# Two blocks of transformers in fp32: the order of the gate and up products of 256 tokens, and where the context's modulation is summed

## The reference

```python
def swiglu_ffn(h, w_in, w_out):
    gate, up = jnp.split(h @ w_in, 2, axis=-1)
    return (jax.nn.silu(gate) * up) @ w_out
...
    for l in range(DEPTH):
        x = x + FFN_RESID * swiglu_ffn(rms_norm(x, ffn1_norm[l]), ffn1_w_in[l], ffn1_w_out[l])
...
        x = x + FFN_RESID * swiglu_ffn(rms_norm(x, ffn2_norm[l]), ffn2_w_in[l], ffn2_w_out[l])
...
    s_c = jax.nn.silu(c)
    s_cc = jax.nn.silu(c_ctx)[None]
    for i in range(DEPTH):
        ml = (s_c @ w_mod[i] + b_mod[i]).reshape(-1, 3, 3, D)
        mc = (s_cc @ w_mod[i] + b_mod[i]).reshape(-1, 3, 3, D)
```

## Time and profile before

| | us |
|---|---|
| median of 3 runs | 3210.66 (3208.84 to 3212.32) |
| the profiled execution | 3210.62 |
| its span, first to last instruction | 3208.8 |
| PE busy | 3145.6, 98% |
| DVE busy | 1988.8, 62% |
| ACT busy | 1360.5, 42% |
| POOL busy | 129.1, 4% |
| granted TensorE clock, mean | 0.995 |

### The profile page before, as it was taken

One profiled execution on the slowest core, in us unless ns is written; L12 is line 12 of the kernel. 1 busy time (PEld: TensorE's weight loads), 2 busy tenths in 40 slices (PEclk: granted clock), 3 DMA queues, 4 the chain that ended last, 5 costly groups with the idle time before them and its releaser, 6 DMA issues.

```text
span 3208.8 us, 39761 instructions
## 1 busy us (share of the span) xinstructions
PE 3145.6 (98%) x15550; PEld 2625.7 (82%) x15550; DVE 1988.8 (62%) x2775; ACT 1360.5 (42%) x1907; POOL 129.1 (4%) x160
## 2 busy tenths in 40 slices
PE   8999999999999999999999999999999999999998
PEld 7888888888888887888878888788887788887787
DVE  7968778778687787763344444776335643345665
ACT  6546655455566555322233333323223322245553
POOL 1000000000000000000000000300000000021000
PEclk9999999999999999999999999999999999999999
DMA  8755366667554676542332222354324633253354
GB/s 255 246 192 180 124 197 223 223 224 242 162 182 135 201 237 205 190 157 93 105 99 79 79 92 80 105 171 152 111 92 158 211 117 106 91 139 91 105 188 154
DMA packets 334901, 496.78 MB, mean 155 GB/s; under 512 B 11042, under 2 KB 221884, under 8 KB 334716
## 3 DMA queue, kind: packets, MB, share of 16 engines
q1 hardware_dynamic: 330652, 483.46, 45.5%
q0 software_dynamic: 4064, 10.77, 1.5%
HBM read 493.09 MB, written 1.10 MB: 154 GB/s over the span
## 4 chain that ended last, share of the span: by engine, by line
PE 94%; DVE 3%; issue 1%; ACT 1%; DMA 0%; POOL 0%; SPq 0%; DVEq 0%; POOLq 0%; ACTq 0%
PE bank L567 23%; PE bank L569 23%; PE bank L568 23%; PE bank L623 13%; PE bank L624 7%; PE bank L582 1%; PE bank L738 1%; PE bank L753 0%; PE bank L1032 0%; DVE wlo L1715 0%; DMA raw<-in_w_in_dram 0%; DVE bank L2550 0%; PE bank L590 0%; POOL small L2618 0%; ACT npr L1663 0%
## 5 line engine op out<-in xcount | busy, mean ns | idle before, releaser
L1715 DVE TENSOR_TENSOR wlo<-raw,whi 128x1024 fp32r<-128x1024 f32 (+1 forms) x780 | 940.0, 1213 | 899.2 <-ACT whi L1198 896.9
L1198 ACT ACTIVATE whi<-raw 128x1024 fp32r<-128x1024 f32 (+1 forms) x780 | 815.7, 1050 | 1154.1 <-PE bank L569 990.3
L623 PE MATMUL bank<-xT,whi 128*128 128x512 f32 x1760 | 621.8, 398 | 1.5 <-DVE xT L1796 1.0
L567 PE MATMUL bank<-xTh,whi 128*128 128x512 f32 (+1 forms) x1312 | 509.0, 388 | 6.9 <-DVE xTl L1796 6.7
L569 PE MATMUL bank<-xTh,wlo 128*128 128x512 f32 (+1 forms) x1312 | 505.0, 385 | 0.0
L568 PE MATMUL bank<-xTl,whi 128*128 128x512 f32 (+1 forms) x1312 | 504.8, 385 | 0.0
L624 PE MATMUL bank<-xT,wlo 128*128 128x256 f32 x1760 | 496.2, 282 | 0.0
L623 PEld LDWEIGHTS bank<-xT,whi 128*128 128x128 f32 x1760 | 333.1, 189 | 82.1 <-issue 3.4
L567 PE MATMUL bank<-whi,hh 128*128 128x512 f32 x968 | 378.3, 391 | 0.0
L569 PE MATMUL bank<-whi,hl 128*128 128x512 f32 x968 | 377.2, 390 | 0.0
L568 PE MATMUL bank<-wlo,hh 128*128 128x512 f32 x968 | 377.0, 389 | 0.0
(11 more groups left out here) (383 smaller groups left out, 3653.0 us busy)
## 6 DMA issues: line engine op xcount, KB each, us to landing
raw<-in_ffn_w_in_dram SPq DMA_DIRECT2D x176, 1024.0 KB, 5.2
raw<-in_ffn_w_out_dram SPq DMA_DIRECT2D x80, 1024.0 KB, 5.1
mraw<-in_w_mod_dram SPq DMA_DIRECT2D x72, 1024.0 KB, 5.1
raw<-in_w_in_dram SPq DMA_DIRECT2D x44, 1024.0 KB, 5.2
raw<-in_ret_w_in_dram SPq DMA_DIRECT2D x24, 1024.0 KB, 5.1
raw<-in_w_branch_dram SPq DMA_DIRECT2D x12, 1024.0 KB, 5.1
raw<-in_nat_w_qkv_dram SPq DMA_DIRECT2D x12, 1024.0 KB, 5.2
raw<-in_ffn_w_out_dram SPq DMA_DIRECT2D x16, 512.0 KB, 3.4
```

The costliest lines, as they stand in the source:

```text
L567: pe.matmul(ps, lh, rh, start=start, stop=False, skip_group_check=True)
L623: pe.matmul(ps[:, :], wh[:, k, :], x, start=k == 0, stop=False, skip_group_check=True)
L1198: nc.scalar.activation(hi, src, ACT.Copy).then_inc(*e.inc("hi", key, part))
L1715: nc.vector.tensor_tensor(lo, src, hi.bitcast(F32), ALU.subtract).then_inc(*e.inc("lo", key, part))
```

## The change

It does two things. In `feature_pairs` a part's eight 512-column products (`mm_high`, which waits for whi alone) now come before its eight 256-column ones (`mm_low`, ahead of which PE waits for wlo); with `norm` all high products of both parts come as xT arrives, then the low ones of one part and of the other. And in f1 and f2 VectorE accumulates only `who` 0 of the modulation, in one place per step (`mod_steps`, after `ahead`). For `who` 1 ScalarE multiplies (k = 0 straight into `macc`, else into a new buffer `mprod`) and GpSimd adds. TensorE's sums wait for both (`mod_step`, `mod_other`), SP's modulation loads for both readers. The adds are put into GpSimd's list after the norm of f1 (before the one of the mixers) and after that of f2.

```diff
+        mprod = arena("mprod", [P, D], 24 * KB)
...
                             sp.wait_ge(*e.at("mod_read", q - 2))
+                            if mods.halves[q - 2][0][0][0] == "f":
+                                sp.wait_ge(*e.at("mod_read_too", q - 2))
...
                     pe.wait_ge(*e.at("mod_step", c, KD - 1))
+                    if name[0][0] == "f":
+                        pe.wait_ge(*e.at("mod_other", c, KD - 1))
...
-                order = [(mc, k) for mc in range(2) for k in range(KD)]
+
+                def begun(mc):
+                    pe.wait_ge(*e.at("hi", key, mc))
+                    w[mc] = part_views(key, mc)[1:]
+                    ps[mc] = new(*u, mc, ring="pairs")
+
                 if norm:
                     order = [(0, 0), (0, 1), (1, 0), (1, 1)] + [(mc, k) for k in range(2, KD) for mc in range(2)]
-                for mc, k in order:
-                    if norm and mc == 0:
-                        pe.wait_ge(*e.at("xT", norm, k))
-                    if mc not in w:
-                        w[mc] = split_ready(key, mc)
-                        ps[mc] = new(*u, mc, ring="pairs")
-                    m = mm2(ps[mc], k, *w[mc])
-                    if k == KD - 1 and mc == 0:
+                    for mc, k in order:
+                        if mc == 0:
+                            pe.wait_ge(*e.at("xT", norm, k))
+                        if mc not in w:
+                            begun(mc)
+                        mm_high(ps[mc], k, w[mc][0])
+                for mc in range(2):
+                    if not norm:
+                        begun(mc)
+                        for k in range(KD):
+                            mm_high(ps[mc], k, w[mc][0])
+                    pe.wait_ge(*e.at("lo", key, mc))
+                    for k in range(KD):
+                        m = mm_low(ps[mc], k, w[mc][1])
+                    if mc == 0:
                         m.then_inc(*e.inc("used", key, mc))
-                    elif k == KD - 1:
+                    else:
                         m.then_inc(*e.inc(*u, also=[("used", key, mc)]))
...
+            def mod_products(name, at):
+
+                for c, k, q in mods.steps.get((name, at), ()):
+                    act.wait_ge(mod_landed[q % 2], 16 * (q // 2 + 1))
+                    if c + k == 0:
+                        act.wait_ge(*e.at("scc"))
+                    read = [("mod_read_too", q)] if k % 2 else []
+                    if k == 0:
+                        if c >= 2:
+                            act.wait_ge(*e.at("modp", c - 2))
+                        A(macc[c % 2][:, 1, :], mraw[q % 2][:, 0, :], ACT.Copy, scale=scc[:, k, 1:2])\
+                            .then_inc(*e.inc("mod_other", c, 0))
+                    else:
+                        if k > 1:
+                            act.wait_ge(*e.at("mod_other", c, k - 1))
+                        elif c:
+                            act.wait_ge(*e.at("mod_other", c - 1, KD - 1))
+                        A(mprod[:, :], mraw[q % 2][:, k % 2, :], ACT.Copy, scale=scc[:, k, 1:2])\
+                            .then_inc(*e.inc("mod_product", c, k, also=read))
+
...
                         high(g - 1)
+                    mod_products(name, 2 * g)
...
                     A(sg[:, g % 2, :], sg[:, g % 2, :], ACT.Silu).then_inc(*e.inc("sg", name, g, 0))
+                    mod_products(name, 2 * g + 1)
...
                         down_ahead(until, name, n, d)
+                        if name[0][0] == "f":
+                            mod_products(name, 22 + 6 * n + d)
...
-                    for who in whos_of(c):
+                    for who in range(1) if name[0][0] == "f" else whos_of(c):
                         a, wk, s = macc[c % 2][:, who, :], mraw[q % 2][:, k % 2, :], scc[:, k, who:who + 1]
...
-                    mod_half(name, 2 * g, 0)
+                    mod_steps(name, 2 * g)
...
-                    mod_half(name, 2 * g, 1)
                     ahead(until, (name, "up", g))
-                    mod_half(name, 2 * g + 1, 0)
+                    mod_steps(name, 2 * g + 1)
...
                     behind(until, (name, "up", g))
-                    mod_half(name, 2 * g + 1, 1)
...
+            def mod_other(c):
+
+                for k in range(1, KD):
+                    pool.wait_ge(*e.at("mod_product", c, k))
+                    pool.wait_ge(*e.at("mod_other", c, k - 1))
+                    a = macc[c % 2][:, 1, :]
+                    nc.gpsimd.tensor_tensor(a, a, mprod[:, :], ALU.add).then_inc(*e.inc("mod_other", c, k))
+
...
                     norm(("f1", l), 256)
+                for c in MOD_PARTS["f1", l]:
+                    mod_other(c)
                 norm(("mx", l), 256)
...
                 norm(("f2", l), 256)
+                for c in MOD_PARTS["f2", l]:
+                    mod_other(c)
```

More of the change, by code:

```diff
@@ L618, in feature_major_arriving, with mm_high, mm_low @@
                                 m.then_inc(*e.inc(*also[0]))
-            def mm2(ps, k, wh, wl):
+            def mm_high(ps, k, wh):
                 x = xT256[:, k, :, :].rearrange("p a t -> p (a t)")
                 pe.matmul(ps[:, :], wh[:, k, :], x, start=k == 0, stop=False, skip_group_check=True)
+            def mm_low(ps, k, wl):
                 return pe.matmul(ps[:, 256:512], wl[:, k, :], xT256[:, k, 0, :], start=False, stop=k == KD - 1,
@@ L1830, in turned_y @@
                             m.then_inc(*e.inc("yT", name, c, frees=("ty", name, u) if j == n - 1 else None))
[L1832 to L1847, removed]
             def mod_steps(name, at):
```

## The result

| | before | after |
|---|---|---|
| median, us | 3209.97 (3205.09 to 3213.18, 9 runs) | 3217.34 (3216.78 to 3219.91, 9 runs) |
| span of the profiled execution, us | 3208.8 | 3215.5 |
| VectorE busy, us | 1988.8 | 2018.9 |
| ScalarE busy, us | 1360.5 | 1425.2 |
| GpSimd busy, us | 129.1 | 293.9 |

The change makes the kernel slower: ratio 1.0027, 95% interval 1.0018 to 1.0035. The forecast was 3212 us; the time lies in the range of 3204 to 3221, on the side of rival (c). VectorE, which gave away 64 instructions, is busier than before.

The account below looks back on a forecast made before the run. TensorE was taken to bound the kernel, over 94% of the span, so only its products' pitch could yield time. 0 - 4.6 + 5.9 + 0 = +1.3 us on 3210.6 us gave 3212 us, range 3204 to 3221.

Parts of the forecast that it names:

- rival (c): f1 and f2, slabs 22 to 27: GpSimd's adds make wlo late, L624 or L569 waiting; 3224 us, 20%.
- VectorE gives work away, GpSimd adds: Modulation sums in f1 and f2: 78 us off VectorE and 56 adds of 2.4 us on GpSimd, priced at 0.
- The sum is 5.9 us behind: Slabs 20 to 26: VectorE falls back 0.7 us in five down slabs, 1.25 us in two gate and up slabs.
- cover: Lead of a wlo: 3 parts of 2.72 us less 1.06 and 1.22 us, 5.9 us, judged just enough.
- the bound: If a 0.69 us VectorE instruction doesn't overlap the add in two slabs: 1.4 us in four FFNs, 5.6 us.
- The order of the products: 220 parts: 27 ns lost per change from 256 to 512 columns, 0 for the reverse, 5.9 us lost.
- The slow rhythm: About 690 alternating pairs in f2 of layer 0, f1 of layer 1: 6.6 ns each, 4.6 us gained by blocks.
- The later wait for lo: PE asks for lo 1.8 us later: taken as 0, up to 0.5 us at each of five FFN starts.
- ScalarE's products: 64 products of 1024 columns at 1.15 us, 74 us in all, expected to lie in ScalarE's idle time.
- SP's and PE's new waits: SP waits for ScalarE's mraw reads, PE's sum for the last add: SP no later, the add 11 us ahead.
- the half-clock stretches: After the norms: one stretch costs about 1.7 us, and two more or less are possible either way.
- No wait of PE on wlo: Sign of a right forecast: PE waits on none of wlo, macc or whi in the five FFNs.

Follow-up runs that it names:

- the kernel with short adds: The changed kernel with each GpSimd add on 64 of 1024 columns, ScalarE's products and all waits kept: 3209.25 us, ratio 1.0004 to the kernel before.
- the order alone: The kernel before with only the new order of products, the modulation sums staying on VectorE: 3209.32 us, ratio 1.0002 to the kernel before.

## Why the prediction was right or wrong

**The number: in the range, by the width of the range.** The sum gave 1.3 us more than before; the medians differ by 7.4. The range held the time because it was drawn as far as rival (c), and (c), at 20%, is what happened.

**VectorE gives work away, GpSimd adds: wrong, and this is the step that failed**, in "The sum is 5.9 us behind", "5.9 us" of cover, "It just fits. I take 0". The mechanism, the instructions that it strikes, the place (slabs 22 to 27) and the sign (a product of the down stage waiting for wlo; it was L570, L567 before, and not the L569 that I named) were all there, as rival (c). The term itself was mis-sized: nothing in the sum, 7.4 us measured. Both sides of the balance were missed. The cover is 5.6 us (the kernel with short adds). The backlog is 7.0: without the stall PE would have read the part at 158.84 + 0.23 = 159.07, the split ended at 160.5, 1.4 us too late, and 5.6 us of lead were gone. I had spread the holds evenly, one to a slab of 5.44 us, 0.7 us behind each. The accumulations start at 140.53, 148.06, 155.90 and 161.57 us, 7.5, 7.8 and 5.7 us apart, 4.7 us behind in three slabs where I had 2.1. The first interval still holds the last group's sum, product and hl; the second has two holds, since ScalarE made its next product at 150.51, as soon as GpSimd was free, and two adds started 3.7 us apart. The price is 1.8 to 1.9 us at each of four places, 7.4, against 0 in the sum and 5.6 as the bound. A balance of two numbers that are equal to a tenth is no reason for 0: a miss on either side costs, and none gains.

**The order of the products: mechanism right, size 1.5 us off.** From 256 to 512 columns 27 ns was right (1.84 us for eight against 8 x 0.2267). From 512 to 256, where I took 0 and excluded a gain, the eight take 0.95 us against 0.96, and sixteen 1.91 against 1.92: 7 ns are won. 20 ns x 220 = 4.4 us instead of 5.9.

**The slow rhythm: right that blocks don't fall into it; wrong to book it as a property of two FFNs.** In the profile before it cost 4.6 us; in another execution it lies elsewhere, in a similar number of pairs, so the 4.6 us are an estimate from one draw. Its gain and the price of the widths nearly cancel, and the order alone agrees with that (ratio 1.0002). One correction to my rows: the earlier trace rows stand in f2 of layer 0 (f1 of layer 1 begins only at 647 us); the pair of FFNs named in the text is the right one.

**The later wait for lo, ScalarE's products, SP's and PE's new waits: right**, nothing in time that can be measured. The products take 1.13 us (I took 1.15). ScalarE waited 2.7 us for GpSimd, in 4 places; an add that comes first lasts 2.4 us, as I took.

**What would show it**: the parts of 2.80 us, the eights at 0.227 and 0.120 us, the lengths of wlo and of the adds came as forecast. "No wait of PE on wlo" did not, and the sign named for (c) is the row that appeared. (c) gave 3217.6 us for the late wlo alone; the time is 3217.34. That the two are so close is partly luck: the stalls cost 1.8 us more than (c) had them, the widths 1.5 and the half-clock stretches 1.2 us less.

## What to carry to other kernels

Before work is moved from VectorE to GpSimd, count what GpSimd reads: while it reads SBUF, VectorE's instructions with two inputs there stand still, and here 56 adds of 2.4 us cost VectorE 96 us to relieve it of 66. Where steps have room between them this cost nothing that could be measured, and where they follow each other it eats a lead until the bounding engine waits; draw up the queue of the tightest stretch instruction by instruction, with the helper's instructions as close together as their waits allow. If lead and backlog come out equal, expect the stall.

## What was not expected of the hardware

- A change from 512 to 256 columns in a stream of products gains about 7 ns (sixteen of 256 in 1.91 us, against 0.120 each), while the one back costs 27.
- The alternation of a 512 and a 256-column product has two rhythms, 2.773 and 2.82 to 2.83 us for eight pairs, and the same program takes one or the other in the same FFN from one execution to the next. In blocks of eight or sixteen only one was seen, in ten kernels. What sets it was not found.
